# A diffusion trunk: twenty modulation pairs instead of twelve in the hybrid units, their loads issued by GpSimd

## The reference, cut to what matters

```
s_lat = jax.nn.silu(c)[:, None, :]
for layer in range(DEPTH):
    mod = jnp.split(s_lat @ mod_w[layer] + mod_b[layer], 6, axis=-1)
    h = modulate(rms_norm(x, norm_mix_pre[layer]), mod[0], mod[1])
    ...
    x = x + mod[2] * rms_norm(y, norm_mix_post[layer])
    h = modulate(rms_norm(x, norm_ffn_pre[layer]), mod[3], mod[4])
    x = x + mod[5] * rms_norm(conv_ffn(h, ...), norm_ffn_post[layer])
```

## Time and profile before

| | us |
|---|---|
| median of three runs | 1811.05 |
| profiled execution | 1826.54 |
| its span | 1824.7 |
| TensorE busy | 1727.2 (95%) |
| VectorE busy | 986.7 (54%) |
| ScalarE busy | 686.7 (38%) |
| GpSimd busy | 340.5 (19%) |

### The profile page before, as it was taken

How to read it: one execution, slowest core, us unless ns; L and a number is a source line. 1 busy time by engine, 2 the same in 40 slices (tenths; PEclk the granted TensorE clock), 3 DMA queues, 4 the chain that set the end, 5 groups by cost and what they waited for, 6 DMA issues and landing times.

```text
span 1824.7 us, 22554 instructions
## 1 busy us (share of the span) xinstructions
PE 1727.2 (95%) x9080; PEld 1435.1 (79%) x9080; DVE 986.7 (54%) x1248; ACT 686.7 (38%) x1010; POOL 340.5 (19%) x227
## 2 busy tenths in 40 slices
PE   8899999988988999889999999999999999999998
PEld 2688788888988956567888888887888788888886
DVE  2644439777687566757544444346446744444232
ACT  2443523333322276733433333232223244343321
POOL 3047303443143054512000000110002100000000
PEclk9899899999999867999999999999999899999999
DMA  8326440110111023032223322321322122332221
GB/s 335 114 79 193 110 150 24 47 47 24 47 47 47 1 92 115 24 93 88 74 92 102 105 89 84 107 90 48 109 98 93 46 93 92 97 109 88 87 85 65
DMA packets 153918, 161.14 MB, mean 88 GB/s; under 512 B 11383, under 2 KB 151144, under 8 KB 152680
## 3 DMA queue, kind: packets, MB, share of 16 engines
q1 hardware_dynamic: 153344, 159.74, 27.1%
q10 hardware_dynamic: 488, 0.18, 0.0%
HBM read 157.81 MB, written 2.10 MB: 88 GB/s over the span
## 4 chain that ended last, share of the span: by engine, by line
PE 83%; DVE 9%; ACT 3%; issue 2%; POOL 2%; DMA 0%; SPq 0%; DVEq 0%; ACTq 0%; POOLq 0%
PE ps L483 17%; PE ps L485 17%; PE ps L484 17%; PE ps L724 4%; PE ps L745 3%; PE ps L750 3%; ACT mod_raw_c L1131 1%; PE ps L834 1%; PE ps L538 1%; PE ps L851 1%; PE ps L873 1%; PE ps L808 1%; PE ps L852 1%; PE ps L853 1%; DVE w_lo L1423 1%
## 5 line engine op out<-in xcount | busy, mean ns | idle before, releaser
L1423 DVE TENSOR_TENSOR w_lo<-w_raw,w_hi 128x2048 fp32r<-128x2048 f32 x100 | 234.1, 2342 | 485.3 <-ACT w_hi L1077 485.3
L483 PE MATMUL ps<-h_hi,w_hi 128*128 128x512 f32 x968 | 380.2, 393 | 2.1 <-DVE w_lo L1423 2.1
L484 PE MATMUL ps<-h_lo,w_hi 128*128 128x512 f32 x968 | 379.3, 392 | 0.0
L485 PE MATMUL ps<-h_hi,w_lo 128*128 128x512 f32 x968 | 378.7, 391 | 0.0
L1077 ACT ACTIVATE w_hi<-w_raw 128x2048 fp32r<-128x2048 f32 x100 | 191.2, 1913 | 309.7 <-PE ps L485 272.3
L483 PEld LDWEIGHTS ps<-h_hi,w_hi 128*128 128x128 f32 x968 | 183.2, 189 | 40.5 <-DVE w_lo L1423 2.6
L485 PEld LDWEIGHTS ps<-h_hi,w_lo 128*128 128x128 f32 x968 | 183.3, 189 | 38.8
L484 PEld LDWEIGHTS ps<-h_lo,w_hi 128*128 128x128 f32 x968 | 183.3, 189 | 37.7
L1956 POOL TENSOR_TENSOR mod_raw_c<-mod_raw_c 128x1024 f32<-128x1024 f32 (+2 forms) x84 | 132.4, 1576 | 170.8 <-ACT mod_raw_c L1131 166.2
L2013 POOL TENSOR_TENSOR sum_acc_y<-sum_acc_y,sum_y 128x512 f32<-128x512 f32 x18 | 27.0, 1501 | 592.6 <-ACT sum_y L1307 592.6
L483 PE MATMUL ps<-mid_hi,w_hi 128*128 128x512 f32 x338 | 132.9, 393 | 0.0
(11 more groups left out here) (337 smaller groups left out, 2920.5 us busy)
## 6 DMA issues: line engine op xcount, KB each, us to landing
w_raw<-in_ffn_w_up SPq DMA_DIRECT2D x44, 1024.0 KB, 5.1
mod_raw_c<-in_mod_w SPq DMA_DIRECT2D x28, 1024.0 KB, 5.3
w_raw<-in_ffn_w_down SPq DMA_DIRECT2D x16, 896.0 KB, 4.7
mod_raw_e<-in_mod_w SPq DMA_DIRECT2D x12, 1024.0 KB, 5.3
w_raw<-in_sc_w_in SPq DMA_DIRECT2D x12, 1024.0 KB, 5.2
w_raw<-in_hyb_w_in SPq DMA_DIRECT2D x9, 1024.0 KB, 7.9
mod_raw_a<-in_mod_w SPq DMA_DIRECT2D x8, 1024.0 KB, 16.0
w_raw<-in_ffn_w_down SPq DMA_DIRECT2D x8, 1024.0 KB, 5.0
```

What stands on the lines that cost most here:

```text
L483: mm(dst, hi, xh[:, k0 + k, :], start=first and k == 0, stop=False)
L484: mm(dst, hi, xl[:, k0 + k, :], start=False, stop=False)
L485: i = mm(dst, lo, xh[:, k0 + k, :], start=False, stop=last and k == nk - 1)
L1423: V.tensor_tensor(wlo[s][:, :], raw[s][:, :], f32(whi[s][:, :]), ALU.subtract).then_inc(sem("w_lo"), 1)
```

## The change

Two numbers change: `EARLY` from 12 to 20 and `LEVEL_PAIRS` from 12 to 4. So pairs 0 to 19 are early, with products at the end of units 1 to 10; pairs 20 to 23 are in the levels, and `mod_at` puts their products at level 1 of steps 0 to 3, sums at level 3 and columns at level 5. The loads of early pairs are issued by GpSimd: that of pair j + 2 right after the sums of pair j. TensorE takes the columns of pairs 16 to 19 after the rows of the norms.

```
-        EARLY, LEVEL_PAIRS = 12, 12
+        EARLY, LEVEL_PAIRS = 20, 4
...
         def mod_at(q, lag):
 
-            return [j for j in range(EARLY, EARLY + LEVEL_PAIRS) if 3 * (j - EARLY) + lag == q]
+            return [j for j in range(EARLY, EARLY + LEVEL_PAIRS) if LEVELS * (j - EARLY) + 1 + lag == q]
...
-            def load_early(j):
-
-                if j == 0:
-                    sp.wait_ge(sem("h"), 2 * KC)
-                elif j >= 2:
-                    sp.wait_ge(sem("mod_acc"), acc_c(j - 2))
-                sp.dma_start(mraw_e[j % 2][:, :, :], mod_source(j)).then_inc(sem(f"mod_e{j % 2}"), 16)
...
-                for j in early_at(u - 2):
-                    load_early(j)
...
-            for u in range(U_WOUT - 2, U_WOUT + 2):
-                for j in early_at(u):
-                    load_early(j)
...
-            for u in range(U_WOUT - 3, U_WOUT + 3):
+            for u in range(U_WOUT - 3, U_WOUT):
                 mod_columns(early_at(u))
...
             pool.wait_ge(sem("h"), KC)
+            def load_early(j):
+
+                if j >= 2:
+                    pool.wait_ge(sem("mod_acc"), acc_c(j - 2))
+                pool.dma_start(mraw_e[j % 2][:, :, :], mod_source(j)).then_inc(sem(f"mod_e{j % 2}"), 16)
+
+            pool.wait_ge(sem("h"), 2 * KC)
+            load_early(0)
+            load_early(1)
             for j in range(EARLY):
                 mod_parts(j)
+                if j + 2 < EARLY:
+                    load_early(j + 2)
```

More of the change, by code:

```diff
@@ L212, in u_count, with mod_source @@
             return (s * (LEVELS - 1) + l) * 2 + d + 1
+        def mod_source(j):
+            layer, part = divmod(8 + j, MODS // 2)
+            return A["mod_w"][layer].rearrange("(k p) n -> p k n", p=P)[:, :, part * UW:(part + 1) * UW]
         def mod_block(i, lag):
@@ L352, in _ @@
             sp.dma_start(vrow[V_CCTX:V_CCTX + KC, 0, :], A["c_ctx"].rearrange("(c p) -> c p", p=P)).then_inc(sem("c_in"), 16)
-            def mod_source(j):
-                layer, part = divmod(8 + j, MODS // 2)
-                return A["mod_w"][layer].rearrange("(k p) n -> p k n", p=P)[:, :, part * UW:(part + 1) * UW]
-            def load_early(j):
-                if j == 0:
-                    sp.wait_ge(sem("h"), 2 * KC)
-                elif j >= 2:
-                    sp.wait_ge(sem("mod_acc"), acc_c(j - 2))
-                sp.dma_start(mraw_e[j % 2][:, :, :], mod_source(j)).then_inc(sem(f"mod_e{j % 2}"), 16)
             def load_mod_pair(j):
```

## The result

The changed kernel took **1851.37 us** (median of four runs, 1839.49 to 1859.95) against 1812.54 us for the kernel before (median of four runs beside it). The ratio is 1.0186, with a 95% interval of 1.014 to 1.0233. The likeliest case, no change at 1813 us, was wrong. The time fell between the cases, inside the range and on the side of "slower", which had 0.42.

A forecast was written before the change was run, and what follows sets the result against it. TensorE holds 83% of the chain of waits; in later hybrid units the load, product and sum loop is slower. Losing 15 us there and saving 13 in the DeltaNet gave +2 us, 1813 us at the median; range 1798 to 1872.

The forecast's parts named there:

- The likeliest case: Whole kernel, rival A: g near 1.5 us, 1813 us, no change, own range 1803 to 1829; chance 0.46.
- The DeltaNet levels: DeltaNet steps: eight pairs leaving them save 13 us, with bounds of 7 and 21 us.
- bad collisions: DeltaNet steps 3 and 4: two pairs' sums beside the first block masks cost 6.8 us, which the change removes.
- SyncE's waits for sums: SyncE's load queue: 95.4 us of waits for GpSimd's sums, with weights queued behind, disappear; no gain credited.
- g: Hybrid units: time one load issue holds GpSimd and delays its load; taken as 1.5 us, between 0.37 and 5.3.
- Rival B: Early loads: GpSimd writes row addresses in software, held nearly until landing; g 5.3 us, 1871 us; chance 0.26.
- rival C: Early loads: each issue is held by one VectorE product or split of 2.3 us; g 3.8, 1845 us; chance 0.10.
- my sum: Whole kernel: 15 us lost in the hybrid units, 13 us saved in the DeltaNet, +2 us net, 1813 us.
- sums of 6.5 us: Hybrid units: GpSimd's sums of most pairs take 6.5 us, even and odd in turn, within a 16.6 us round.
- The tail: From VectorE's last eviction to the small product releasing the DeltaNet: 16.1 us, some 1.6 us of it done earlier.
- the clock as a risk: TensorE's granted clock, 0.64 in the first attention stretch: the forecast is wrong if it moves.
- +15 for the hybrid units: Hybrid units: eight more pairs in 16.6 us rounds delay the DeltaNet's release from 265.96 to 281.0 us, 15 us lost.

The follow-up runs named there:

- e11: Twelve early and twelve level pairs, GpSimd issuing, VectorE's odd early product cut to 16 of 2048 columns; ratio 0.9962 to the kernel before.
- e12: The kernel before (twelve early pairs, SyncE issuing) with VectorE's odd early product cut to 16 of 2048 columns; ratio 0.9978 to the kernel before.
- e4: The changed kernel with VectorE's gate work ahead of its product and four early-pair buffers instead of two; ratio 0.9974 to the kernel before.
- e6: Twenty early pairs, gate work first and four buffers as in e4, but SyncE issues the early loads; ratio 1.0006 to the kernel before.
- e2: Twenty early pairs, two buffers, VectorE's gate work first, as e1, but SyncE issues the early loads; ratio 1.0019 to the kernel before.
- e7: e1 with VectorE's product of each odd early pair cut to 16 of 2048 columns; ratio 1.0023 to the kernel before.
- e1: The changed kernel with VectorE's gate work (abt copy, g) ahead of its own pair product; 1846.24 us, ratio 1.0126 to the kernel before.
- e3: The kernel before with only the queue part: GpSimd issues the early loads, twelve early and twelve level pairs; 1827.55 us, ratio 1.0074.
- e5: The kernel before with only the split: twenty early and four level pairs, SyncE issuing, gate work behind the product; ratio 1.0066.
- e9: e8 with VectorE's last odd product moved behind the second scaled tile in the tail; 1798.91 us, ratio 0.9924 to the kernel before.
- e8: e4 with SyncE's bulk loads for the level pairs held until the last early load has landed; ratio 0.9996 to the kernel before.

## Why the prediction was wrong in its likeliest case

**What held.** The DeltaNet levels: forecast 13 us less, measured 12.1, inside the bounds of 7 and 21. The four kernels with twelve level pairs show 373 to 376 us from release to the first score, the ten with four show 360 to 363. The placement of the bad collisions was read well: from first mask to level 2 takes 6.3 us in steps 3 and 4. SyncE's waits for sums went, and the changed kernel shows no gain from it, as credited; e11 against e12 and e4 against e6 have the release 2.3 and 2.5 us sooner without them. The issue: g was 1.5 us by choice. It held GpSimd for 0.30 + 0.90 us. Landing counts from the start of the issue, 5.9 us against 5.3, so the even loop itself grew by 0.30 + 0.6 = 0.9 us; the 1.8 us of my expectation for e2 count the 0.90 us twice. Rival B, which needed 2.85, and rival C, with 3.8, were wrong in their mechanism: the longest of twenty issues took 1.05 us. I drew rival C from the Trainium skill, same page and section, and stretched it. The page has such a load's descriptors starve beside a two-port operation of VectorE, as an f32 copy; for an instruction with two SBUF inputs, as products and splits are here, it has the lock only against a GpSimd instruction that reads SBUF. No run here shows starving for this load.

**Luck.** That 1851.37 us lies inside my range is owed to rivals B and C, 1871 and 1845 us. By its own terms my sum was 38 us short, and neither rival's mechanism is there.

**What failed: sums of 6.5 us.** That term of the round, taken from the earlier trace rows, was the step that broke. I had written that most sums take 6.5 us, even and odd in turn. The even sums took 8.2 to 8.5 us in six of the first seven rounds of the changed kernel, the odd ones 4.6. I had seen the two engines shut each other out, and took their present mean as a constant of both. It is not one: the total for both parities hardly moves, but nearly all of the stretching now falls into the even buffer's loop, which is the one that sets the pace. e7, e11 and e12 show this. The trace of before had it once already, in its last round: pair 10's sum took 8.42 us and pair 11's 4.67, beside the product of 4.48 us that I had read the earlier trace rows.

```profile
191.97 5.67 POOL L1956 TENSOR_TENSOR mod_raw_e<-mod_raw_e 128x1024 f32<-128x1024 f32 x2 [5.30 <-ACT mod_raw_e L1131]
197.78 2.61 POOL L1956 TENSOR_TENSOR mod_sums<-mod_raw_e 128x256 f32<-128x256 f32 x1
200.35 3.80 POOL L1956 TENSOR_TENSOR mod_raw_e<-mod_raw_e 128x1024 f32<-128x1024 f32 x2
```

It made the even rounds 18.4 us on average, the long one aside, instead of 16.6: over nine rounds some 16 us.

**What was missing: the order in units 8, 9 and 11.** I followed the loop's two buffers and not what is queued behind a late product on VectorE. Three things are: the copy of abt, g, and the evictions of aq. I counted the last alone. The first is the bubble of 31.1 us; e1 shows it at 12.5 us of the release, 3.9 of them in the tail.

**The tail, carried over at its 16.1 us.** It grew to 25.9 us. The granted clock was 0.84 in 250 to 270 us, 0.67 in 270 to 290 and 0.59 in 290 to 310, while before it was 1.00 from 250 to 266 us; the steps L1556 came every 4.27 us instead of 2.23. All profiles fit this: 2.23 us a step in before, e3, e5, e11 and e12, whose clock was 1.00 at these steps, and 4.27 in the changed kernel, e1, e4 and e6 to e9, where it was 0.50 to 0.58. What lowered the clock is open: in 270 to 290 us TensorE was busy for only 13.5 of 20 us, but e9 had a low clock without such a gap. I had named the clock as a risk, but for the attention.

**The sum.** Forecast +15 for the hybrid units, measured +52.1: about 12 for the bubble, 10 for the tail, some 16 for the longer even rounds, and close to the forecast 15 for the rest. These are shares of one path and overlap by a few us. With SyncE as issuer and the gate work first the sum was close: at 0.37 us it has the last eviction of e2 at 262.0 us, as measured, and only the longer tail makes 17.3 us out of its 11. Some of that is luck, since two of e2's rounds took 21.9 and 13.1 us. By parts of the change: the split alone +11 net and the queue alone +14, the two together +40 at the first score.

## What to carry to other kernels

When work is moved into a loop that already sets the pace, do not carry the mean of two alternating durations into it: ask which of the two lies in the buffer's loop, and whether a shift of a few us between the engines would stretch that one and spare the other. Before adding late loads to an engine's program, list what stands behind each wait that needs no load, and put that first; here this order cost 12 us in one place and about 9 in another. A queue of its own for loads did no harm once there were buffers to run ahead with: 22 us lost at the release with two, none with four (2.5 us sooner, in one profile of each).

## What the chip showed that I had not expected

- A 1 MB load issued by GpSimd held it for 0.90 us and landed 5.9 to 6.4 us after the start of its issue (medians of eight kernels), against 5.2 to 5.3 us by SyncE (six kernels).
- VectorE's product of 2048 columns takes 2.29 us, or 4.36 us when GpSimd's addition of 1024 columns began 0.17 us ahead of it; the three additions of a pair take 4.57 us alone and 8.4 us when a product and a split of VectorE fall in them.
- Beside six 1 MB loads of SyncE, at 344 to 346 GB/s in all, a load landed 10.1 us after the start of its issue (e4); with those held back it was 8.5 us (e8).
- In e4 the clock fell to 0.50 while TensorE idled for 13 us, and stood there from 256 to 264 us, in which TensorE was busy throughout. In e9 it fell to 0.50 with TensorE busy for the 14 us ahead, and before the change it was 0.57 from 236 to 240 us in the same way.
- One kernel's runs differ by more than its edits: beside e1 to e4 the kernel before took 1804.7 to 1830.5 us in 24 of its 25 runs, and the granted clock went with it, 0.973 in the fastest and 0.956 in the slowest.
